# Expert outputs added to the residual rows in DRAM by the scatter, and a shorter last stage

## Chip, core and metric

One Trainium2 chip, one core. The metric is the device time of one execution in microseconds. The kernel before takes 815.87 us as the median of 3 runs (814.08 to 816.09).

## What is computed

One layer of a hybrid encoder for 512 prompt tokens and 32 sample tokens (544 rows of 1024 f32): a modulated RMS norm, a projection into two groups of heads (a gated linear recurrence and a forgetting attention), an output projection with a gated residual, then a grouped mixture of experts with a gated residual and a last RMS norm. The change touches what comes after the output projection:

```
def moe(h, w_router, b_router, w_gate, w_up, w_down):
    ...
    y = jnp.zeros((B * L, D), jnp.float32)
    for e in range(N_EXPERTS):
        he = jax.nn.silu(t @ w_gate[e]) * (t @ w_up[e])
        y = y + gates[:, e:e + 1] * (he @ w_down[e]).astype(jnp.float32)
    return y.reshape(B, L, D).astype(h.dtype)

    # in trunk_layer: x is the residual after the output projection ("x2"), h its modulated norm ("h2")
    x = x + gate_f * moe(h, p['w_router'], p['b_router'], p['w_exp_gate'][l], p['w_exp_up'][l], p['w_exp_down'][l])
    # at the end: rms_norm(x, final_norm_gain)
```

There are 16 experts of width 512; each token goes to exactly 2 of them. An expert's three weight matrices are 6.3 MB in f32, so all experts are 100 MB.

## The kernel before, in words

**Routing.** `route` (line 1098, on DVE) ranks the experts of each token, counts the tokens of each expert (a PE step, "pos"), and gives each of the 1088 token-expert pairs a place in a list of tiles of 32 rows, at least 2 tiles an expert. One-hot matrices (`row_hot`, `tile_hot`, `tile_entry`, lines 1163 to 1168) and 20 matmuls ("tab", line 2019) turn that into `tseq`, a table that holds for each tile two indices: the row of `h2_d` to gather from and the row of `y_d` to write to. `h2_d` holds the 544 rows of h2 in DRAM; `y_d` has 1088 rows, the first expert's output of a token in its first half, the second's in its second. A further 20 matmuls ("gates", line 2028) make the router's weight of each place.

**The tile loop.** This input has 44 tiles. A tile's 32 tokens stand on 128 partitions, four quarters of 256 elements a token. For tile t:

- POOL issues the gather, an indirect DMA of 128 rows of 1 KB (line 838), two tiles ahead of its use, into one of two buffers.
- DVE rearranges them (`reorder_rows`, line 1561), and transposes them (`turn_rows`, line 1565) when PE is done with the tile before.
- PE multiplies with the gate and up weights (line 2042, 128 matmuls recorded as 64), ACT applies silu (line 1084), DVE multiplies (line 1580) and transposes the product (line 1588).
- PE multiplies with the down weights (line 2053), behind the next tile's gate and up matmuls.
- DVE multiplies the result with the router's weight and the modulation gate (lines 1593 to 1597, then the eviction in `y_out`, line 1602) into one of two `ysb` buffers.
- POOL issues the scatter (line 844) of 128 rows of 1 KB to `y_d`.

The order on each engine is written out by hand. DVE, in pass t: turn rows t+1, hidden product t, **reorder rows t+2**, factors, transpose hidden t, evict y t-1. POOL, in turn: gather n+4 (after DVE has reordered n+2), scatter n (after its eviction, and after the scatter from the same buffer, n-2, has landed). PE: gate and up of t, then down of t-1.

**Weights.** SP loads experts in 6 pieces of 1 MB, each issued when the piece four before it has landed, into 4 expert buffers. The loads of expert e wait for the last tile of expert e-4.

**The last stage.** SP loads x2 rows of row tiles 0 and 4 while the last tiles run. When all scatters have landed it loads 10 pieces of `y_d` (lines 651 and 652), two for each of the 5 row tiles. For row tiles 0 and 4 DVE adds them to x2; for 1, 3 and 2 PE adds them with an identity matrix (line 2085) onto x2, which 12 matmuls at line 2001 put in PSUM just after routing began. ACT squares and sums, DVE takes the root (`rstd`, three Newton steps) in three groups, and scales; SP stores.

Of the kernel before, what the change touches and what calls it, by code (L numbers as in the profile page):

```python
# [18 lines left out]
I32 = mybir.dt.int32  # L19
# [19 lines left out]
MAXT = 2 * NE + 2 * TOK // ET  # L39
# [22 lines left out]
def build(nc, a, out):  # L62
    ctx = ExitStack()
    with ctx:  # L64
# [109 lines left out]
        y_d = dram("y_d", (2 * TOK, D))  # L174
# [105 lines left out]
        grp("tab", 6, "dve")  # L280
        grp("gates", 6, "dve")
# [76 lines left out]
        s_xsum = sem("x2_in_psum")  # L358
        s_xr = sem("x2_reloaded")
# [116 lines left out]
        gA, gB = view(R, T0 + 912, NTILE), view(R, T0 + 920, NTILE)  # L476
# [8 lines left out]
        quarter_i = view(R, T0 + 1050, 1).bitcast(I32)  # L485
        quarter = view(R, T0 + 1443, 1)
        quarter_out = view(R, T0 + 1051, 1)
# [6 lines left out]
        entry = view(R, T0 + 1464, 2 * NTILE, 2)  # L494
        iota_r = view(R, T0 + 1484, P)
        iota_t = view(R, T0 + 1484 + P, MAXT + 2)

        tseq = view(XH, 8960, MAXT + 2, 2).bitcast(I32)
        row_hot = view(R, 1920, 2 * NTILE, P)
        tile_hot = view(R, 3200, 2 * NTILE, MAXT + 2)  # L500
        tile_entry = view(R, 0, 2 * NTILE, MAXT + 2, 2)

        ya = [view(W, 6 * SLOT + n * D, D) for n in range(NTILE)]
        yb = [view(W, 6 * SLOT + (NTILE + n) * D, D) for n in range(NTILE)]
        gateF = view(XH, 8192, 2, QD)
# [52 lines left out]
        def _(sp):  # L558
# [39 lines left out]
            first_pieces(0, (2, 3))  # L598
            first_pieces(1, (0, 1))
# [41 lines left out]
            for i in (0, 4):  # L641
                sp.dma_start(xr[i][0:ROWS[i], :], x2_d[i * P:i * P + ROWS[i], :]).then_inc(s_xr, 16)
# [5 lines left out]

            def load_y(i):
                n = ROWS[i]  # L650
                sp.dma_start(ya[i][0:n, :], y_d[i * P:i * P + n, :]).then_inc(s_ya[i], 16)  # L651
                sp.dma_start(yb[i][0:n, :], y_d[TOK + i * P:TOK + i * P + n, :]).then_inc(s_ya[i], 16)  # L652

            for i in FIN:
                load_y(i)
            for m, i in enumerate(FIN):
                n = ROWS[i]
                sp.wait_ge(s_fin, m + 1)
                sp.dma_start(out["y_prompt"][0, i * P:i * P + n, :] if i < 4 else out["y_sample"][0],
                             ya[i][0:n, :]).then_inc(s_out[m % 2], 16)  # L660
# [8 lines left out]
        def _(pool):  # L669
# [140 lines left out]
            g.iota(iota_r, [[0, P // ET], [1, ET]], base=0, channel_multiplier=0, allow_small_or_imprecise_dtypes=True)  # L810
            g.iota(quarter_i, [[0, 1]], base=0, channel_multiplier=1)
            g.iota(iota_t, [[1, MAXT + 2]], base=0, channel_multiplier=0, allow_small_or_imprecise_dtypes=True)
            for c in range(2):
                g.iota(entry[:, c * NTILE:(c + 1) * NTILE, 0], [[P, NTILE]], base=-8 * TOK, channel_multiplier=1,
# [1303 lines left out]
```

## Time and profile before

| what | value |
|---|---|
| median of 3 runs | 815.87 us |
| the profiled execution, its own time | 812.85 us |
| its span | 811.1 us |
| PE busy | 688.7 us (85%) |
| DVE / ACT / POOL busy | 382.1 / 207.5 / 203.9 us |
| routing, first one-hot matrix to the first gate matmul | 485.1 to 504.4 us |
| tile loop, first gate matmul to the last eviction | 504.4 to 776.2 us |
| last stage, last scatter landed to the end | 779.4 to 811.1 us |

Times inside the profile count from the start of the span. 1.8 us of the execution lie outside the span. PE, DVE, ACT, POOL and SP run on their own and wait for each other through semaphores; a wait shows as idle time of an engine before an instruction, with the instruction or DMA that ended it.

### The profile page before, as it was taken

How to read it: one execution, taken by the hardware profiler on the slowest of the kernel's cores; microseconds unless marked ns; L12 is line 12 of the kernel's file. 1: busy time of each engine (PE TensorE's matmuls, PEld its weight loads, DVE VectorE, ACT ScalarE, POOL GpSimd, SP SyncE). 2: the span in 40 equal slices, each digit the busy share in tenths (PEclk: the TensorE clock that was granted, in tenths of full speed). 3: DMA queues.
4: the chain of work that ended last, by engine and by line, in shares of the span. 5: the costliest groups of instructions: out<-in, count | busy, mean ns of one | idle time of the engine just before them, and what ended most of it. 6: DMA issues, size and time to landing. Idle time of an engine off the chain costs nothing. (4 is left out here: it accounts for less than half of the span.)

```text
span 811.1 us, 18872 instructions
## 1 busy us (share of the span) xinstructions
PE 688.7 (85%) x7369; PEld 434.6 (54%) x7370; DVE 382.1 (47%) x1063; ACT 207.5 (26%) x429; POOL 203.9 (25%) x338
## 2 busy tenths in 40 slices
PE   3699999999787789998899955998889988979925
PEld 1385485444244678666645534665556655656712
DVE  4200025011497898666635483344445444455546
ACT  5300145001422142566111100222222232223202
POOL 1212200001842610311000001343334344434410
PEclk9799999999989999998799975999999999999978
DMA  8953074364104100950770187899995999972053
GB/s 330 390 236 104 26 286 183 130 227 176 68 17 144 45 2 6 330 187 5 306 304 27 49 321 304 323 416 416 417 418 204 415 421 413 415 321 97 30 194 155
DMA packets 37540, 179.59 MB, mean 221 GB/s; under 512 B 5816, under 2 KB 6216, under 8 KB 21808
## 3 DMA queue, kind: packets, MB, share of 16 engines
q1 hardware_dynamic: 29536, 157.31, 49.0%
q0 software_dynamic: 7952, 21.55, 7.6%
q8 instruction: 38, 0.62, 0.3%
q14 instruction: 14, 0.11, 0.0%
HBM read 168.00 MB, written 13.71 MB: 224 GB/s over the span
## 5 line engine op out<-in xcount | busy, mean ns | idle before, releaser
L1754 PE MATMUL bank<-weights,x_hT 128*128 128x512 f32 x256 | 113.3, 601 | 0.0
L1738 PE MATMUL bank<-x_hT,weights 128*128 128x272 f32 x384 | 91.7, 400 | 2.0 <-DMA weights<-in_w_in 2.0
L2042 PE MATMUL bank<-weights,R 128*32 128x256 f32 x1408 | 83.1, 388 | 11.9 <-DVE R L1565 5.7
L1738 PEld LDWEIGHTS bank<-x_hT,weights 128*128 128x128 f32 x384 | 73.9, 194 | 18.5 <-DMA weights<-in_w_in 2.4
L1754 PEld LDWEIGHTS bank<-weights,x_hT 128*128 128x128 f32 x256 | 48.7, 193 | 60.3 <-issue 60.1
L844 POOL DMA_INDIRECT y_d<-R,x_hT x44 | 45.1, 1024 | 123.6 <-DVE R L1602 110.1
L2042 PEld LDWEIGHTS bank<-weights,R 128*32 128x32 f32 x1408 | 54.7, 112 | 37.3 <-issue 10.8
L1084 ACT ACTIVATE R<-bank 128x128 f32<-128x128 f32 x44 | 12.2, 277 | 205.7 <-PE bank L2042 205.7
L1084 ACT ACT_TABLE_LOAD x44 | 56.5, 1283 | 22.6 <-DVEq L1191 21.8
L838 POOL DMA_INDIRECT R<-h_d,x_hT x46 | 49.2, 1070 | 37.6 <-POOL x_hT L856 32.1
L1964 PE MATMUL bank<-weights,x_hT 128*128 128x512 f32 x128 | 56.9, 596 | 0.0
L1561 DVE COPY R<-R 128x256 f32 (+1 forms) x46 | 18.6, 404 | 75.0 <-DMA R<-h_d,x_hT 72.8
L2053 PE MATMUL bank<-R 128*32 128x256 f32 x704 | 44.2, 391 | 9.4 <-DVE R L1602 9.2
L2053 PE MATMUL bank<-weights,R 128*32 128x256 f32 x704 | 42.6, 380 | 9.3 <-DVE R L1602 9.2
L2042 PE MATMUL bank<-R 128*32 128x256 f32 x704 | 40.3, 379 | 3.1 <-issue 3.1
L2042 PE MATMUL bank<-x_hT,R 128*32 128x256 f32 x704 | 40.3, 379 | 2.5 <-issue 2.5
L2053 PEld LDWEIGHTS bank<-R 128*32 128x32 f32 x704 | 26.8, 112 | 24.3 <-issue 15.6
L2053 PEld LDWEIGHTS bank<-weights,R 128*32 128x32 f32 x704 | 25.8, 109 | 24.2 <-issue 15.5
L1565 DVE STREAM_TRANSPOSE R<-R 128x256 f32<-128x256 f32 x45 | 20.1, 446 | 38.5 <-PE bank L2042 36.5
L1964 PEld LDWEIGHTS bank<-weights,x_hT 128*128 128x128 f32 x128 | 23.6, 190 | 26.4 <-issue 26.3
L1718 PE MATMUL bank<-weights,cpad 128*32 128x512 f32 x192 | 25.0, 648 | 14.7 <-DMA weights<-in_w_ada 14.7
L1266 DVE COPY weights<-bank 128x272 f32<-128x272 f32 x8 | 3.2, 437 | 70.4 <-PE bank L1738 70.2
(353 smaller groups left out, 997.2 us busy)
## 6 DMA issues: line engine op xcount, KB each, us to landing
weights<-in_w_ada SPq DMA_DIRECT2D x24, 1024.0 KB, 11.8
weights<-in_w_exp_gate SPq DMA_DIRECT2D x16, 1024.0 KB, 10.2
weights<-in_w_exp_down SPq DMA_DIRECT2D x16, 1024.0 KB, 10.4
weights<-in_w_exp_up SPq DMA_DIRECT2D x16, 1024.0 KB, 10.9
R<-in_w_exp_down SPq DMA_DIRECT2D x16, 1024.0 KB, 10.5
weights<-in_w_in SPq DMA_DIRECT2D x7, 2048.0 KB, 8.8
R<-in_w_exp_up SPq DMA_DIRECT2D x8, 1024.0 KB, 10.7
R<-in_w_exp_gate SPq DMA_DIRECT2D x8, 1024.0 KB, 10.4
```

The source lines that it names most:

```text
L838: pool.indirect_dma_start(xg[:, par * QD:(par + 1) * QD], None, h2_quarters, bass.IndirectOffsetOnAxis(ap=gather_rows[par], axis=0), bound ...
L844: pool.indirect_dma_start(y_quarters, bass.IndirectOffsetOnAxis(ap=scatter_rows[par], axis=0), ysb[:, par * QD:(par + 1) * QD], None, boun ...
L1084: A.activation(hs, bank[2][:, 0:P], ACT.Silu).then_inc(s_sil, 1)
L1266: read("dve", f"hf{h}{c}", V.tensor_copy(fr[:, c * HALF:(c + 1) * HALF], bank[4 + 2 * (h % 2) + c][:, 0:HALF]))
L1561: V.tensor_copy(xsort, xg[:, bass.ds(place * QD, QD)].rearrange("p (r b) -> p b r", b=KT)).then_inc(s_xs, 1)
L1565: V.transpose(XT.rearrange("p b r -> p (b r)"), xsort.rearrange("p b r -> p (b r)")).then_inc(s_xt, 1)
L1718: ins = T.matmul(bank[b][32 * j:32 * j + 32, :], cpad[:, k, :], w[:, j * 512:(j + 1) * 512], start=(k == 0), stop=(k == KT - 1))
L1738: ins = T.matmul(bank[b][:, 0:HALF], w[:, k, h * P:(h + 1) * P], hT[:, k, c * HALF:(c + 1) * HALF], start=(n == 0), stop=(n == KT - 1))
L1754: ins = T.matmul(bank[b][:, :], hT[:, k, i * P:(i + 1) * P], w[:, k, :], start=(k == 0), stop=(k == KT - 1))
L1964: ins = T.matmul(b[:, :], hT[:, k, i * P:(i + 1) * P], wslot(f"wo{k // 2}", D)[:, k % 2, c * 512:(c + 1) * 512], start=(k == 0), stop=(k = ...
L2042: ins = T.matmul(bank[2][32 * j:32 * j + 32, 0:2 * P].rearrange("p (w f) -> p w f", w=2), XT[:, k, :], W2[:, :, k, j * P:(j + 1) * P], sta ...
L2053: ins = T.matmul(bank[6][32 * j:32 * j + 32, 0:QD], heT[:, f, :], Wd[:, f, j * QD:(j + 1) * QD], start=(f == 0), stop=(f == FT - 1))
```

## The change

- `y_d` is gone. All five x2 row tiles are stored to `x2_d` (before, two). The scatter goes to `x2_d` with `compute_op=ALU.add`, so that the DMA adds the 128 rows to what is there.
- Since both experts of a token now add to the same row, each scatter waits for the scatter before it to have landed, not for the one before that.
- Gather and scatter use one index, so `tseq` and the one-hot matrices are smaller: 32 columns in place of 128. The table comes out on 32 partitions and DVE writes it in four pieces. The first two gathers take their index from `tseq` itself and start when it has been written.
- In the DVE loop `reorder_rows(t + 2)` stands behind `y_out(t - 1)`.
- SP issues the 8 gate broadcasts earlier, and the first piece of expert 2's gate weights only when the first two gathers have landed.
- The last stage loads 5 pieces of `x2_d`. DVE multiplies them with the gain while ACT squares, one root for all five, then DVE scales three row tiles and ACT two. PE has no part; the 12 matmuls at line 2001 and the 12 adds at line 2085 (24 rows in the profile) are gone.

```
-MAXT = 2 * NE + 2 * TOK // ET
+MAXT = 2 * NE + 2 * TOK // ET - 2
...
+            for gi in range(2):
+                for j in range(4):
+                    sp.dma_start(gateF[32 * j:32 * j + 32, gi, :], bcast(mod_d[gi, 5 * D + j * QD:5 * D + (j + 1) * QD], 32)).then_inc(s_ph3, 16)
             first_pieces(1, (0, 1))
...
-            sp.wait_ge(s_x2w, 32)
-            sp.wait_ge(s_xsum, 1)
+            sp.wait_ge(s_x2w, 16 * NTILE)
             first_pieces(3, (2, 0, 1))
             both(sp, s_h2w)
+            for n in range(2):
+                sp.wait_ge(s_gath[n], 16)
             first_pieces(2, (0,))
...
-            def load_y(i):
...
             for i in FIN:
-                load_y(i)
+                sp.dma_start(xr[i][0:ROWS[i], :], x2_d[i * P:i * P + ROWS[i], :]).then_inc(s_xr[i], 16)
...
             def scatter(par):
                 pool.sem_inc(s_begun, 1)
-                pool.indirect_dma_start(y_quarters, bass.IndirectOffsetOnAxis(ap=scatter_rows[par], axis=0),
+                pool.indirect_dma_start(x2_quarters, bass.IndirectOffsetOnAxis(ap=scatter_rows[par], axis=0),
                                         ysb[:, par * QD:(par + 1) * QD], None,
-                                        bounds_check=last_y, oob_is_err=False).then_inc(s_yst[par], 16)
+                                        bounds_check=last_quarter, oob_is_err=False, compute_op=ALU.add).then_inc(s_yst[par], 16)
...
             def next_scatter(u, par):
-                if not isinstance(u, int):
-                    pool.wait_ge(s_yst[par], u * 16)
-                g.tensor_copy(scatter_rows[par], tseq[:, bass.ds(u * 2 + par, 1), 1]).then_inc(s_idx, 1)
+                g.tensor_copy(scatter_rows[par], tseq[:, bass.ds(u * 2 + par, 1)]).then_inc(s_idx, 1)
                 pool.wait_ge(s_ye, u * 2 + (par + 2))
+                if par:
+                    pool.wait_ge(s_yst[0], u * 16 + 16)
+                elif not isinstance(u, int):
+                    pool.wait_ge(s_yst[1], u * 16)
...
-            V.tensor_tensor(row_hot, iota_r.unsqueeze(1).broadcast_to([P, 2 * NTILE, P]),
-                            dst_r.unsqueeze(2).broadcast_to([P, 2 * NTILE, P]), ALU.is_equal)
...
+            vlink(dve, V.tensor_tensor(row_hot, iota_r.unsqueeze(1).broadcast_to([P, 2 * NTILE, ET]),
+                                       dst_r.unsqueeze(2).broadcast_to([P, 2 * NTILE, ET]), ALU.is_equal))
+            V.tensor_tensor(row_entry, row_hot, entry.unsqueeze(2).broadcast_to([P, 2 * NTILE, ET]), ALU.mult)
+            V.tensor_tensor(tile_hot, iota_t.unsqueeze(1).broadcast_to([P, 2 * NTILE, MAXT + 2]),
+                            dst_t.unsqueeze(2).broadcast_to([P, 2 * NTILE, MAXT + 2]), ALU.is_equal).then_inc(s_oh, 1)
...
@@ hidden(t)
-                reorder_rows(t + 2, t % 2)
@@ block.vector
             with dve.Fori(5, total) as t:
                 hidden(t)
                 gate_factors(t)
...
                 y_out(t - 1, (t - 1) % 2)
+                reorder_rows(t + 2, t % 2)
...
+            for m, i in enumerate(FIN):
+                n = ROWS[i]
+                dve.wait_ge(s_xr[i], 16)
+                V.tensor_tensor(yr[i][0:n, :], xr[i][0:n, :], fing[0:n, :], ALU.mult).then_inc(s_gain, 1)
+            dve.wait_ge(s_fsq, NTILE)
+            rstd(st[:, 105:110], st[:, 100:105], D)
+            dve.wait_ge(s_gain, NTILE)
+            dve.sem_inc(s_root, 1)
+            for m in (0, 2, 4):
+                n = ROWS[FIN[m]]
+                y = yr[FIN[m]][0:n, :]
+                V.tensor_scalar(y, y, st[0:n, 105 + m:106 + m], None, ALU.mult).then_inc(s_fin["dve"], 1)
```

On POOL, the second half of the loop's body, before. `rows_reordered` is DVE's step at line 1561, `y_evicted` the one at line 1602, `y_stored0` and `y_stored1` tell of landed scatters from the two buffers:

```order
L856 ISA [waits rows_reordered]
L856 COPY x_hT<-x_hT 128x1
L879 REGISTER_ALU
L838 DMA R<-h_d,x_hT 128x256 [waits index_copied]
L862 ISA [waits y_stored1]
L862 COPY x_hT<-x_hT 128x1
L863 REGISTER_ALU
L882 REGISTER_ALU [waits y_evicted]
L844 DMA y_d<-R,x_hT 4352x256 [waits index_copied]
```

The same place in the changed kernel:

```order
L835 ISA [waits rows_reordered]
L835 COPY x_hT<-x_hT 128x1
L860 REGISTER_ALU
L816 DMA R<-h_d,x_hT 128x256 [waits index_copied]
L839 ISA
L839 COPY x_hT<-x_hT 128x1
L840 REGISTER_ALU
L842 REGISTER_ALU [waits y_evicted]
L863 REGISTER_ALU [waits y_stored0]
L822 DMA x_d<-R,x_hT 2176x256 [waits index_copied]
```

The wait for a landed scatter has moved from ahead of the index copy to just ahead of the scatter, and from the same buffer's last scatter (two tiles back) to the other buffer's (one tile back).

On DVE, the loop's body before, from the hidden product on:

```order
L1580 TENSOR_TENSOR R<-R,bank 128x32x4 [waits silu_done,xT_ready]
L1558 ISA
L1560 ISA [waits rows_gathered0]
L1561 ISA [waits rows_gathered1]
L1561 COPY R<-R 128x256
L1593 ISA [waits rows_reordered]
L1593 COPY stats<-R 128x2
...
L1588 STREAM_TRANSPOSE R<-R 128x128 [waits down_done,hidden_ready,gate_factor_step]
L1621 ISA [waits hiddenT_ready]
L1622 ISA [waits y_stored0]
L1602 ISA [waits y_stored1]
L1602 TENSOR_TENSOR R<-bank,x_hT 128x256
```

And in the changed kernel:

```order
L1555 TENSOR_TENSOR R<-R,bank 128x32x4 [waits silu_done,xT_ready]
L1567 ISA
L1567 COPY stats<-R 128x2
...
L1562 STREAM_TRANSPOSE R<-R 128x128 [waits down_done,hidden_ready,gate_factor_step]
L1599 ISA [waits hiddenT_ready]
L1600 ISA [waits y_stored0]
L1576 ISA [waits y_stored1]
L1576 TENSOR_TENSOR R<-bank,x_hT 128x256
L1533 ISA
L1535 ISA [waits rows_gathered0]
L1536 ISA [waits rows_gathered1]
L1536 COPY R<-R 128x256
```

The wait for the gathered rows of tile t+2 stood ahead of the factors, the hidden transpose and the eviction; it now stands behind all three.

## Rows read from the trace of the kernel before

**Rows 1.** The page: span, busy time of each engine.
```profile
span 811.1 us, 18872 instructions
PE 688.7 (85%) x7369; PEld 434.6 (54%) x7370; DVE 382.1 (47%) x1063; ACT 207.5 (26%) x429; POOL 203.9 (25%) x338
```
**Rows 2.** Scatters (line 844) in stretches of the loop: us, POOL busy (x count), PEclk, DMA share, GB/s.
```profile
515.50:616.50 101.00, 16.42 (x16) 0.98 1.00 406
...
625.70:726.60 100.90, 16.68 (x17) 1.00 0.99 403
726.60:769.00 42.40, 7.18 (x7) 1.00 0.21 67
```
**Rows 3.** POOL in time order, 651 to 663 us: start, us, instruction, idle before.
```profile
651.96 1.06 POOL L838 DMA_INDIRECT R<-h_d,x_hT  x1 [0.79 <-POOL x_hT L856]
656.15 1.02 POOL L844 DMA_INDIRECT y_d<-R,x_hT  x1 [2.94 <-DVE R L1602]
658.17 1.06 POOL L838 DMA_INDIRECT R<-h_d,x_hT  x1 [0.79 <-POOL x_hT L856]
662.46 1.02 POOL L844 DMA_INDIRECT y_d<-R,x_hT  x1 [3.03 <-DVE R L1602]
```
**Rows 4.** DVE in time order, the same stretch.
```profile
658.64 0.40 DVE L1561 COPY R<-R 128x256 f32 x1 [2.42 <-DMA R<-h_d,x_hT]
661.14 0.42 DVE L1602 TENSOR_TENSOR R<-bank,x_hT 128x256 f32 x1 [0.53 <-DVE R L1588]
664.58 0.40 DVE L1561 COPY R<-R 128x256 f32 x1 [1.94 <-DMA R<-h_d,x_hT]
```
**Rows 5.** Waits of DVE, 515 to 727 us: total, times, longest.
```profile
DVE R L1561 <- DMA R<-h_d,x_hT: 63.2, 31, 3.5
```
**Rows 6.** PE in time order after the weights have landed, 727 to 766 us.
```profile
727.23 3.66 PE L2042 MATMUL bank<-weights,R 128*32 128x256 f32 x64 [0.71 <-issue]
...
760.55 3.66 PE L2042 MATMUL bank<-x_hT,R 128*32 128x256 f32 x64
765.73 3.66 PE L2042 MATMUL bank<-x_hT,R 128*32 128x256 f32 x64
```
**Rows 7.** The chain that ended last: the last scatter.
```profile
777.07 2.36 DMA y_d<-R,x_hT
```
**Rows 8.** Routing, 474 to 504 us, in time order.
```profile
473.86 0.49 DVE L1114 TENSOR_TENSOR R<-R 128x320 f32<-128x320 f32 x1
485.11 1.48 DVE L1163 TENSOR_TENSOR R<-R 128x1280 f32<-128x1280 f32 x1
486.51 0.86 DVE L1165 TENSOR_TENSOR R<-R 128x680 f32<-128x680 f32 x1
487.40 1.57 DVE L1167 TENSOR_TENSOR R<-R 128x1360 f32<-128x1360 f32 x1
489.12 4.00 PE L2019 MATMUL bank<-R 128*128 128x136 f32 x20 [8.43 <-DVE R L1167]
493.24 0.36 DVE L1189 TENSOR_SCALAR x_hT<-bank,R 128x136 int32<-128x136 f32 x1 [1.07 <-PE bank L2019]
495.85 1.13 POOL L838 DMA_INDIRECT R<-h_d,x_hT  x1 [0.90 <-POOL x_hT L849]
503.44 0.39 DVE L1561 COPY R<-R 128x256 f32<-128x256 f32 x1 [8.77 <-DMA R<-h_d,x_hT]
```
**Rows 9.** The last stage, 779 to 808 us, in time order.
```profile
779.51 0.32 SPq L651 DMA_DIRECT2D weights<-y_d  x1
785.39 1.22 DVE L1635 TENSOR_TENSOR weights<-weights 128x1024 f32<-128x1024 f32 x1 [9.19 <-DMA weights<-y_d]
787.90 1.06 ACT L1096 ACTIVATE weights<-weights 128x1024 f32<-128x1024 f32 x1 [18.17 <-DVE weights L1636]
808.08 0.33 SPq L659 DMA_DIRECT2D out_y_prompt<-weights  x1
```
**Rows 10.** A group by line: a scaling of row tiles, x5, one of them 32 rows.
```profile
L1236 DVE TENSOR_SCALAR weights<-x_hT,stats 128x1024 f32<-128x1024 f32 (+1 forms) x5 | 3.7, 749 | 2.3 <-PE bank L1727 2.2
```

More of the change, by code:

```diff
@@ L279, in build @@
         grp("pos", 6, "dve")
[L280 to L281 removed]
+        grp("tab", 5, "dve")
+        grp("gates", 4, "dve")
         pe_done = sem("pe_done")
@@ L1087, in _ @@
                 n = ROWS[i]
+                act.wait_ge(s_xr[i], 16)
                 if m:
                     act.wait_ge(s_fsq, m)
-                if i in psums:
-                    act.wait_ge(s_part, m - 1)
-                    alink(act, A.activation(jk[0:n, 0:512], bank[psums[i][0]][0:n, :], ACT.Square, accum_out=st[0:n, 100 + m:101 + m]))
-                    A.activation(jk[0:n, 512:D], bank[psums[i][1]][0:n, :], ACT.Square, accum_out=st[0:n, 130 + m:131 + m]).then_inc(s_fsq, 1)
-                else:
-                    act.wait_ge(s_comb, m + 1)
-                    A.activation(jk[0:n, :], xr[i][0:n, :], ACT.Square, accum_out=st[0:n, 100 + m:101 + m]).then_inc(s_fsq, 1)
+                A.activation(jk[0:n, :], xr[i][0:n, :], ACT.Square, accum_out=st[0:n, 100 + m:101 + m]).then_inc(s_fsq, 1)
+            act.wait_ge(s_root, 1)
+            for m in (1, 3):
+                n = ROWS[FIN[m]]
+                y = yr[FIN[m]][0:n, :]
+                A.activation(y, y, ACT.Identity, scale=st[0:n, 105 + m:106 + m]).then_inc(s_fin["act"], 1)
         def route(dve, V, last_h2):
@@ L1183, in route @@
             vlink(dve, V.tensor_tensor(t80[3], t80[3], gts, ALU.mult))
-            V.tensor_reduce(gA, t80[3], AX.X, ALU.add)
+            V.tensor_reduce(weights2[:, 0:NTILE], t80[3], AX.X, ALU.add)
             vlink(dve, V.tensor_tensor(t80[4], gts, t80[3], ALU.subtract))
-            vlink(dve, V.tensor_reduce(gB, t80[4], AX.X, ALU.add))
+            vlink(dve, V.tensor_reduce(weights2[:, NTILE:], t80[4], AX.X, ALU.add))
             filled(dve, "tab")
-            tb = bank[6][:, 0:2 * (MAXT + 2)].rearrange("p (t c) -> p t c", c=2)
-            read("dve", "tab", V.tensor_scalar(tseq, tb, 4.0, quarter_out, ALU.mult, ALU.add))
+            for j in range(P // ET):
+                ins = V.tensor_scalar(tseq[j * ET:(j + 1) * ET, :], bank[5][0:ET, 0:MAXT + 2], 4.0, float(32 * TOK + j), ALU.mult, ALU.add)
+            read("dve", "tab", ins)
             taken(dve, "tab")
             dve.sem_inc(s_rd, 1)
-            for c, weight in ((0, gA), (1, gB)):
-                ins = V.tensor_tensor(tile_hot[:, c * NTILE:(c + 1) * NTILE, :], tile_hot[:, c * NTILE:(c + 1) * NTILE, :],
-                                      weight.unsqueeze(2).broadcast_to([P, NTILE, MAXT + 2]), ALU.mult)
-            ins.then_inc(s_tg, 1)
+            V.tensor_tensor(row_weight, row_hot, weights2.unsqueeze(2).broadcast_to([P, 2 * NTILE, ET]), ALU.mult).then_inc(s_tg, 1)
         @block.vector
@@ L1604, in _ @@
             filled(dve, "gates")
-            read("dve", "gates", V.tensor_copy(row_gate[:, :, 1:], bank[6][:, 0:2 * (MAXT + 2)].rearrange("p (g t) -> p g t", g=2)))
+            for j in range(P // ET):
+                ins = V.tensor_copy(row_gate[j * ET:(j + 1) * ET, :, 1:], bank[4][0:ET, 0:2 * (MAXT + 2)].rearrange("p (g t) -> p g t", g=2))
+            read("dve", "gates", ins)
             taken(dve, "gates")
@@ L1995, in _ @@
             router(4, 1)
-            pe.wait_ge(s_x2, 2 * NTILE)
-            for i, places in psums.items():
-                for c, b in enumerate(places):
-                    taken(pe, last[b])
-                    ins = T.matmul(bank[b][:, :], ident[:, :], x[:, i, c * 512:(c + 1) * 512], start=True, stop=False)
-            ins.then_inc(s_xsum, 1)
             begin("pos")
@@ L2079, in _ @@
             down(3, total)
-            for i in FIN[2:]:
-                places = psums[i]
-                pe.wait_ge(s_ya[i], 32)
-                for c, b in enumerate(places):
-                    for src in (ya, yb):
-                        ins = T.matmul(bank[b][:, :], ident[:, :], src[i][:, c * 512:(c + 1) * 512], start=False, stop=(src is yb))
-                ins.then_inc(s_part, 1)
 _INS = ['x_prompt', 'x_sample', 'cache_fox_k', 'cache_fox_v', 'cache_fox_logf', 'state_hgrn', 'c_prompt', 'c_sample',
```

155 lines of the change are left out of this document (50 added, 105 removed).

## The prediction

> **What bounds the kernel now.** I start from the page: PE is busy 85% of the span [rows 1]. That is a mean over stages with different limits, so I read the three stages that the change touches one by one: routing, the tile loop, the last stage.
>
> For the tile loop I cut the time where the weight stream starts and stops [rows 2]. In two stretches, 201.9 us together, the DMA engines are busy all the time (share 1.00 and 0.99, above 400 GB/s), and 33 scatters begin: 6.12 us a tile. Where the weights are done, one gate-and-up group follows the other every 5.18 us [rows 6]; that is PE's own pace, 5.5 us with the changes of expert (7 intervals from 727.2 to 765.7 us [rows 6]). So in four fifths of the loop PE is not the bound.
>
> What is? The waits say it: in that time DVE waits 31 times, 63.2 us in all, for gathered rows [rows 5]. One gather starts at 651.96 [rows 3], and DVE, which waits for it, starts its reorder at 658.64 [rows 4]: 6.7 us, some 6.2 of it the transfer and the rest DVE's waking and the second wait (the other pairs in this stretch give 6.3 to 6.7). The reader is to see a ring: rows landed, reorder at 658.64, eviction at 661.14 to 661.56, which stands behind the reorder on DVE, scatter 0.90 later at 662.46, then the next gather 2.0 to 2.3 later, then 6.2 again. That is about 12.3 us, and since gathers alternate between two buffers it is 6.15 us a tile. The row count gave 6.12.
>
> **The tile loop after the change.** Two edits work against each other here.
>
> The reorder goes behind the eviction. That cuts the ring: the eviction no longer waits for the gather. A gather would then start some 3 us after the eviction (0.90 + 1.02 + 1.0 [rows 3, 4]) and land 6.2 later, 9.2 us in all, against the two tiles (10.4 us at PE's pace) that it has. The 6.15 us bound is gone, and alone this edit would let the loop run near 5.5 us a tile.
>
> The scatter now waits for the one before it to have landed. It is issued by POOL, so everything behind it on POOL waits too: the next index copy and the next gather. The ring is: scatter starts, lands after L, POOL issues the next one 0.90 after what releases it (661.56 to 662.46 [rows 3, 4]). So the pace is L + 0.9. With nothing else on the DMA engines L is 2.36 us [rows 7], which makes 3.3 us, hidden behind 5.18. But beside the weights no row shows L of a scatter. The nearest row is the gather of the same 128 rows of 1 KB: 6.2 us. The plain write can hardly be much faster than this, since its packets queue behind the same weight packets; I take 5.9 as the lower end. The add must also read the target rows. At the measured 406 GB/s those 128 KB are 0.3 us, and if every row is handled as a transfer of its own the queueing behind weights repeats, which could double the 3.8 us that the load adds (6.2 - 2.4): L up to 10. No row has an add, so this is the term most likely off. I take L = 6.5, near the row: 6.2 + 0.3. The pace is 7.4 us a tile beside the weights.
>
> The weights need the same 201.9 us. In that time there are now 201.9 / 7.4 = 27.3 tiles in place of 33; the other 5.7 follow at 5.5 us: +31 us. Two `ysb` buffers let PE run on for a tile at the start of each stretch and POOL catch up at 3.3 us after it; I estimate 3 us back for each of the two: **+25 us**.
>
> **Routing.** Three one-hot steps of 1.48, 0.86 and 1.57 us become two of 320 elements, 0.49 each, and one of 0.86 [rows 8]: 2.0 us less. The 20 matmuls (4.0 us) get a 32-column stationary operand; I take 2.5, between 2.0 and 4.0, but DVE's other steps behind the one-hots (3.3 us, 488.9 to 492.2) then end last, and four small reads of about 0.25 replace the 0.36 one. So the table is done 2.4 us earlier than 493.60. The gather needs no copy of its index: it starts 0.9 after the table in place of 2.25 (493.60 to 495.85). Together 3.75 us. It took 7.6 us to the reorder at 503.44, with a weight piece and 8 broadcasts just ahead of it on the queues; those are moved, and I take 6.4 as elsewhere: 1.2 more. **-4.9 us**, between -3.7 and -6.5. The 8 broadcasts now take SP 3.7 us near 468 us, where pieces wait for earlier ones anyway. The three more x2 stores are POOL and DMA work before routing, while POOL waits for DVE; the 12 identity matmuls ended at 478.3, before the mask that "pos" waits for at 479.1. I cost all three at nothing. If the DMA engines had no room there, the weight pieces would shift by the 1.5 MB, 3.7 us, ahead of tiles that need them only 20 us later.
>
> **The last stage.** Before: last scatter landed at 779.43, end at 811.1, 31.7 us. After, from the last landing: five issues of 0.45 us on SP, 2.2 MB in place of 4.5. Last piece landed at about +7.8 (2.2 MB at 406 GB/s, and 2.4). ACT squares of 1.06 + 0.2 [rows 9] keep pace, last at +9.1; DVE's gains, 5 of 1.22 [rows 9], end at +9.5. The root is 12 steps of 0.2: +11.9. DVE scales three (0.75 each [rows 10]), ACT two: +14.2. Five stores, 2.2 MB, begin at +12.8, and the DMA needs 5.4 us and a start of 1.7: +19.9. **-11.8 us**, between -9 and -14. The last two scatters began 2.7 us apart (774.37 and 777.07); now the ring of 2.36 + 0.3 + 0.9 = 3.6 spaces them, and the last one itself takes 0.3 more: **+1**.
>
> **Sum**, against the profiled execution's 812.85: -4.9 - 11.8 + 1 + 25 = +9, so 822 us. The runs' median (815.87) lies 3.0 above that execution; on their scale **825 us**. What a measurement can tell from no change is about 0.3%, 2.5 us.
>
> **The rule that speaks the other way.** The trace shows L = 2.36 us without load and 6.2 with it [rows 3, 4, 7]. The Trainium skill ("DMA: Bandwidth & Descriptors", Anatomy of one DMA, SWDGE path) gives one formula for a transfer issued by GpSimd, 2.0 us and the bytes at 436 GB/s, which is 2.3 us here whatever else runs. The row without load agrees, the rows beside the weights do not. By that formula the sum would be the first rival's.
>
> **Rivals.**
>
> *The serial scatter stays hidden, faster.* If a scatter lands within 4.3 us even beside the weights, L + 0.9 is below 5.18 and only the good edit is left. The loop gains perhaps 10 us, not the full 33 x 0.6, since the weight stream (201.9 us) then holds it up. 812.85 - 15.7 - 10 = 787, 790 on the runs' scale. Against it: every gather took 6.2. For it: a write need not wait for a read from DRAM. Chance 0.09.
>
> *The add is free, L = 5.9 to 6.2.* Pace 6.9: 29.3 tiles, 3.7 displaced at 5.5 is 20, less 6, +14. With the other terms 811, and 814 on the runs' scale; with L a little smaller, or more given back by the buffers, 805. This is the point that decides the sign: above L of 6.1 it is slower, below it faster. Chance 0.27, two thirds of it faster.
>
> *The add is dear.* Row by row, L = 8.5: pace 9.4, 21.5 tiles, 11.5 displaced, +63 less 6: 854, 857 on the runs' scale. Then POOL's gathers, queued behind the waiting scatter, come late too. Chance 0.20, from L = 7.5 (843) on.
>
> *My forecast*, L 6.3 to 7.3: 821 to 840. Chance 0.44.
>
> **Numbers.** Faster is the first rival (0.09) and most of the second (0.19): 0.28. Within 0.3%: 0.07, from the second. Slower: 0.65. The range leaves out the first rival and about half of the dear case, 0.19 together: 800 to 852.
>
> **What would show it.** Scatter starts 7 to 8 us apart beside the weights and about 5.2 behind them; POOL's idle time before the scatter ended by the DMA to x2, not by DVE's eviction; DVE's waits for gathers well below 63 us, and its waits before the eviction for a landed scatter instead. First gate matmul near 499.5; from the last landing to the end about 20 us. I am wrong if scatters stay 6.1 apart or closer in the two stretches (then L is smaller than a gather's), or if POOL's scatter instruction itself grows far beyond 1.02 us, which would put the price on POOL and not on the DMA.

## The result, and where the time went

The changed kernel takes **850.1 us** (median of 4 runs, 848.25 to 852.26), the kernel before in the same session 816.0; the ratio is 1.041, 95% interval [1.037, 1.046]. The profiled execution took 851.36 us, span 849.6.

The page and the waits of the changed kernel:

```profile
span 849.6 us, 18805 instructions
PE 684.7 (81%) x7333; PEld 429.8 (51%) x7334; DVE 367.8 (43%) x1037; ACT 209.0 (25%) x425; POOL 229.4 (27%) x336
...
q0 software_dynamic: 12608, 23.13, 10.5%
...
PE 47%; DMA 28%; DVE 11%; issue 7%; ACT 3%; POOL 2%; POOLq 1%; SPq 1%; ACTq 0%; DVEq 0%
```

PE works as long as before (684.7 us against 688.7 [rows 1]), in a longer span. In the chain that ended last, DMA has 28%, and 23% is one kind of transfer, the scatter into x2.

The trace is cut at three instants that every kernel here has: the start of the two "pos" matmuls in routing, the first gate matmul, the landing of the last scatter.

| stage, us | before | after | difference | forecast |
|---|---|---|---|---|
| "pos" to first gate matmul | 25.2 | 21.0 | -4.1 | -4.9 |
| loop, to the last scatter landed | 275.1 | 324.4 | **+49.4** | +26 |
| last stage, to the end | 31.7 | 20.5 | -11.1 | -11.8 |
| sum | | | +34.1 | +9 |

The sum is the difference of the medians (850.1 - 816.0). The two profiles differ by 4.4 us more, because "pos" began at 483.62 in place of 479.21. That is no part of the change: in seven executions of kernels whose code up to there is that of the changed kernel but for a few stores (experiments 1, 2, 5, 6, 7, 9, 10 below), it began between 477.5 and 487.7. Each stage time here and below is that of one profiled execution; the medians are over 4 executions or more.

**The loop.** Scatters (line 822) of the changed kernel in stretches: us, POOL busy (count), PEclk, DMA share, GB/s.

```profile
515.00:605.00 90.00, 16.03 (x10) 0.96 0.97 372
605.00:617.00 12.00, 3.30 (x2) 1.00 0.31 71
617.00:635.00 18.00, 3.19 (x2) 0.81 0.95 365
635.00:650.00 15.00, 4.93 (x3) 1.00 0.34 58
650.00:765.00 115.00, 24.38 (x15) 0.91 0.91 349
765.00:828.00 63.00, 19.11 (x12) 0.98 0.28 45
```

Where before there were 33 scatters in 201.9 us of steady stream [rows 2], there are now 10 in 90 us, and the stream itself has holes: in two of them (605 to 617, 635 to 650) SP waits for a buffer that PE has not released, and between them the granted clock is 0.81. The scatter's own row is in the chain of waits (start, us):

```profile
518.70 9.13 DMA x_d<-R,x_hT
...
528.65 8.88 DMA x_d<-R,x_hT
...
548.88 8.22 DMA x_d<-R,x_hT
...
558.00 8.47 DMA x_d<-R,x_hT
...
820.90 3.63 DMA x_d<-R,x_hT
...
825.38 3.69 DMA x_d<-R,x_hT
```

Beside the weights 16 of them take 8.2 to 9.6 us, mean 8.83; behind the weights 3.4 to 3.9. And POOL, in time order, shows the ring:

```profile
528.65 1.60 POOL L822 DMA_INDIRECT x_d<-R,x_hT  x1 [5.99 <-DVE R L1576]
...
531.25 1.07 POOL L816 DMA_INDIRECT R<-h_d,x_hT  x1 [0.80 <-POOL x_hT L835]
...
538.41 1.60 POOL L822 DMA_INDIRECT x_d<-R,x_hT  x1 [5.89 <-DMA x_d<-R,x_hT]
```

From scatter to scatter 9.8 us: 8.88 until it has landed, then 0.9 until POOL issues the next. The gather goes out 2.6 us behind the scatter. The waits from 515 to 765 us (total, times, longest):

```profile
POOL x_d L822 <- DMA x_d<-R,x_hT: 89.4, 19, 6.6
DVE R L1576 <- DMA x_d<-R,x_hT: 76.6, 24, 6.3
DVE R L1536 <- DMA R<-h_d,x_hT: 38.2, 25, 5.2
PE bank L2000 <- DVE R L1576: 29.8, 14, 4.4
```

DVE waits less for gathered rows, 38.2 us in this stretch of 250 us against 63.2 in one of 212 [rows 5], and twice as long before the eviction (L1576) for a scatter. PE's down matmul waits for that eviction.

**Routing**, in time order:

```profile
483.62 0.71 PE L1957 MATMUL bank<-R 128*128 128x96 f32 x2 [7.88 <-issue]
484.13 2.21 PE L1959 MATMUL bank<-R 128*128 128x80 f32 x10
...
489.85 0.49 DVE L1141 TENSOR_TENSOR R<-R 128x320 f32<-128x320 f32 x1
...
494.84 0.91 DVE L1166 TENSOR_SCALAR x_hT<-bank 32x66 int32<-32x66 f32 x4
...
496.76 1.13 POOL L816 DMA_INDIRECT R<-h_d,x_hT  x1 [9.84 <-issue]
...
503.72 0.39 DVE L1536 COPY R<-R 128x256 f32<-128x256 f32 x1 [7.34 <-DMA R<-h_d,x_hT]
...
504.65 1.94 PE L1989 MATMUL bank<-weights,R 128*32 128x256 f32 x16 [5.74 <-DVE R L1540]
```

One-hots to table: 489.85 to 495.75, 5.9 us, against 8.5 [rows 8]. The gather starts 1.0 us behind the table, against 2.25, and 6.96 us later the reorder begins, against 7.6.

**The last stage**, in time order:

```profile
829.15 2.23 SPq L639 DMA_DIRECT2D weights<-x_d  x5
...
833.30 5.01 DVE L1615 TENSOR_TENSOR weights<-weights 128x1024 f32<-128x1024 f32 x4 [0.59 <-DMA weights<-x_d]
...
837.09 1.06 ACT L1072 ACTIVATE weights<-weights 128x1024 f32<-128x1024 f32 x1
...
840.82 2.07 DVE L1623 TENSOR_SCALAR weights<-weights,stats 32x1024 f32<-32x1024 f32 x3 [0.19 <-DVE stats L1192]
...
841.98 2.99 SPq L643 DMA_DIRECT2D out_y_prompt<-weights  x4
```

The landing is at 829.07; squares end at +9.2, the root at +11.6, scaling at +13.8, the span at +20.5. That is the forecast's schedule, within 0.6 us at every step.

### The profile page after: what moved, and what is told of

Read it like the earlier page. It is cut to its first block, busy times and chain, and to the rows that moved or that the text cites. A ratio compares the mean times of both kernels' runs of the same rounds, so it can differ in the third digit from the quotient of the medians.

```text
span 849.6 us, 18805 instructions
## 1 busy us (share of the span) xinstructions
PE 684.7 (81%) x7333; PEld 429.8 (51%) x7334; DVE 367.8 (43%) x1037; ACT 209.0 (25%) x425; POOL 229.4 (27%) x336
## 3 DMA queue, kind: packets, MB, share of 16 engines
q0 software_dynamic: 12608, 23.13, 10.5%
## 4 chain that ended last, share of the span: by engine, by line
PE 47%; DMA 28%; DVE 11%; issue 7%; ACT 3%; POOL 2%; POOLq 1%; SPq 1%; ACTq 0%; DVEq 0%
DMA x_d<-R,x_hT 23%; PE bank L1693 10%; PE bank L1709 10%; PE bank L1919 6%; PE bank L1989 5%; DMA weights<-in_w_in 2%; PE bank L1673 2%; PE bank L2000 2%; DMA R<-h_d,x_hT 2%; DMA weights<-in_w_ada 1%; PE bank L1638 1%; PE bank L1682 1%; PE bank L1866 1%; PE bank L1712 1%; DVE weights L1342 1%
## 5 line engine op out<-in xcount | busy, mean ns | idle before, releaser
L1709 PE MATMUL bank<-weights,x_hT 128*128 128x512 f32 x256 | 113.0, 600 | 0.0
L822 POOL DMA_INDIRECT x_d<-R,x_hT x44 | 70.9, 1612 | 147.5 <-DMA x_d<-R,x_hT 92.1
L1989 PE MATMUL bank<-weights,R 128*32 128x256 f32 x1408 | 86.1, 399 | 21.7 <-DVE R L1555 12.6
L1989 PEld LDWEIGHTS bank<-weights,R 128*32 128x32 f32 x1408 | 55.2, 115 | 51.0 <-DVE R L1540 21.3
L2000 PE MATMUL bank<-R 128*32 128x256 f32 x704 | 45.5, 400 | 21.0 <-DVE R L1576 21.0
L1919 PE MATMUL bank<-weights,x_hT 128*128 128x512 f32 x128 | 59.5, 618 | 0.0
L1576 DVE TENSOR_TENSOR R<-bank,x_hT 128x256 f32 (+1 forms) x44 | 18.7, 424 | 85.8 <-DMA x_d<-R,x_hT 78.2
L2000 PE MATMUL bank<-weights,R 128*32 128x256 f32 x704 | 45.0, 396 | 10.9 <-DVE R L1576 10.9
L1989 PE MATMUL bank<-R 128*32 128x256 f32 x704 | 44.5, 409 | 7.9 <-DVE R L1555 6.6
L2000 PEld LDWEIGHTS bank<-R 128*32 128x32 f32 x704 | 26.7, 115 | 37.1 <-issue 28.2
L2000 PEld LDWEIGHTS bank<-weights,R 128*32 128x32 f32 x704 | 27.4, 114 | 24.6 <-issue 14.8
L1989 PEld LDWEIGHTS bank<-R 128*32 128x32 f32 x704 | 27.0, 118 | 24.4 <-issue 8.3
## 6 DMA issues: line engine op xcount, KB each, us to landing
weights<-in_w_exp_down SPq DMA_DIRECT2D x16, 1024.0 KB, 11.1
```

The source lines that it names most:

```text
L822: pool.indirect_dma_start(x2_quarters, bass.IndirectOffsetOnAxis(ap=scatter_rows[par], axis=0), ysb[:, par * QD:(par + 1) * QD], None, bou ...
L1576: V.tensor_tensor(ysb[:, bass.ds(place * QD, QD)], bank[6][:, 0:QD], factor, ALU.mult).then_inc(s_ye, 1)
L1709: ins = T.matmul(bank[b][:, :], hT[:, k, i * P:(i + 1) * P], w[:, k, :], start=(k == 0), stop=(k == KT - 1))
L1919: ins = T.matmul(b[:, :], hT[:, k, i * P:(i + 1) * P], wslot(f"wo{k // 2}", D)[:, k % 2, c * 512:(c + 1) * 512], start=(k == 0), stop=(k = ...
L1989: ins = T.matmul(bank[2][32 * j:32 * j + 32, 0:2 * P].rearrange("p (w f) -> p w f", w=2), XT[:, k, :], W2[:, :, k, j * P:(j + 1) * P], sta ...
L2000: ins = T.matmul(bank[6][32 * j:32 * j + 32, 0:QD], heT[:, f, :], Wd[:, f, j * QD:(j + 1) * QD], start=(f == 0), stop=(f == FT - 1))
```

## The experiments

The theory: the loop's pace beside the weights is L + 0.9, and L of an add is 8.8, not 6.5. Rivals: the chain of waits costs by itself, whatever L; the add loads POOL or the DMA engines; the reorder's place matters more or less than thought. All results at once; "loop" and the rest are cut as above, L is the mean over the scatters beside the weights, ratios with 95% intervals.

| kernel | scatter | L | loop | "pos" to gate | last stage | median | ratio to before |
|---|---|---|---|---|---|---|---|
| before | plain, two in flight, reorder ahead | 6.14 | 275.1 | 25.2 | 31.7 | 816.0 | 1 |
| after | add, serial, reorder behind | 8.83 | 324.4 | 21.0 | 20.5 | 850.1 | 1.041 [1.037, 1.046] |
| 1 | plain, serial, behind | 6.27 | 289.0 | 21.1 | 20.5 | 817.1 | 0.999 [0.995, 1.003] |
| 2 | add, two in flight, behind | 8.47 | 257.6 | 20.9 | 20.5 | 779.9 | 0.956 [0.951, 0.961] |
| 3 | before, reorder behind | 6.03 | 253.4 | 24.7 | 31.3 | 794.7 | 0.975 [0.970, 0.980] |
| 4 | before, serial | 6.27 | 293.5 | 25.1 | 33.7 | 843.1 | 1.033 [1.025, 1.041] |
| 5 | add, serial, reorder ahead | 8.89 | 332.4 | 20.9 | 20.6 | 862.1 | 1.057 [1.052, 1.061] |
| 6 | as 1, quarters apart | 6.29 | 290.3 | 21.3 | 21.6 | 818.8 | 1.000 [0.997, 1.004] |
| 7 | as 2, summed, 10 loads | 8.54 | 257.7 | 21.2 | 28.6 | 790.0 | 0.968 [0.964, 0.972] |
| 8 | as 3, with the change's routing | 6.29 | 253.5 | 20.1 | 32.4 | 789.0 | 0.965 [0.962, 0.969] |
| 9 | after, 64 of 128 rows | 7.21 | 301.9 | 20.9 | 20.8 | 827.0 | 1.015 [1.007, 1.022] |
| 10 | 1, 64 of 128 rows | 5.85 | 275.4 | 21.5 | 21.1 | 803.6 | 0.988 [0.981, 0.995] |

L runs from the start of POOL's instruction to the last landing of that scatter, and its mean is over the scatters that take more than three quarters of the longest. The kernel before was run again in every session; its own median was 816.0 beside the changed kernel, 816.3 beside 1 to 4, 818.5 beside 5 to 8 and 812.7 beside 9 and 10, so the ratios compare better than the medians. "pos" to gate repeats within 0.6 us among the kernels with the same code there; the last stage within 1.1 us where it has five loads and within 2.4 us where it is that of before. So these two terms stand on several executions each.

### 1. The add taken away, the serial wait kept

```diff
-  bounds_check=last_quarter, oob_is_err=False, compute_op=ALU.add).then_inc(s_yst[par], 16)
+  bounds_check=last_quarter, oob_is_err=False).then_inc(s_yst[par], 16)
```

> The changed kernel with the scatter writing its rows in place of adding them (it leaves out the sum of the two expert outputs and x2: the last writer of a row stays); the wait for the scatter before and everything else are kept. Theory A (the price is the add itself, which handles the rows one by one, 128 packets of 1 KB in place of 32 of 4 KB): the scatter beside the weights lands after 5.9 to 6.2 us in place of 8.2 to 9.6, POOL's instruction falls from 1.61 to 1.02 us, the pace beside the weights is about 6.9 us a tile in place of 9 to 10, and the time is 812 to 820. Theory B (the price is the chain of waits on POOL, which makes gathers and weight pieces late whatever the scatter does): the scatters stay 8 us apart or more and the time stays above 838.

Theory A holds: 817.1 us, though L (6.27) and the pace (7.21) are a little above what it gave. Chain and page of this kernel:

```profile
558.75 5.99 DMA x_d<-R,x_hT
...
565.62 6.27 DMA x_d<-R,x_hT
```
```profile
q0 software_dynamic: 8384, 23.12, 8.2%
```

The software queue carries 8384 packets against 12608 with the add, 4224 fewer for 44 scatters: 96 each, which is 128 packets against 32; the sizes in the packets' records, 1024 and 4096 bytes, say the same. The add on top of a serial wait costs 35.4 us of loop.

### 2. The add kept, the serial wait taken away

```diff
-  if par:
-      pool.wait_ge(s_yst[0], u * 16 + 16)
-  elif not isinstance(u, int):
-      pool.wait_ge(s_yst[1], u * 16)
...
-  pool.indirect_dma_start(x2_quarters,
+  pool.indirect_dma_start(x2_quarters[par],
```

The scatter two before has to have landed, as in the kernel before, and the second target is a second array, z2_d, a copy of x2.

> The changed kernel with its adds sent alternately to x2 and to a second copy of x2 in DRAM, each scatter waiting only for the one two before it (it leaves out the sum of the two copies, and pays five more stores of x2). Theory A (what costs is that one add stands behind the other, L + 0.9 a tile, while an add in the background is affordable): pace beside the weights 6.1 or below, time 788 to 806. Theory C (the add's single-row packets themselves fill the DMA engines or POOL, however they are ordered): the scatters land later still, 10 us or more, the weight stream falls below 380 GB/s, pace 7 us or more, time above 815.

779.9 us, below theory A's range. Theory C falls. Scatters in the steady stream of this kernel:

```profile
520.00:600.00 80.00, 23.42 (x15) 1.00 1.04 397
660.00:720.00 60.00, 17.56 (x11) 1.00 1.04 396
```

Its adds land as late as those of the changed kernel (8.47), POOL's instruction is 1.6 us as there, and yet a tile takes 5.6 us (35 intervals from 513.2 to 710.9). What is late harms nobody when nobody waits for it. The bill of packets shows only in the stream, 396 to 397 GB/s against 410 to 416 in experiment 3, and in 4.2 us of loop.

### 3. The reorder alone

```diff
 def hidden(t):
...
-    reorder_rows(t + 2, t % 2)
...
     y_out(t - 1, (t - 1) % 2)
+    reorder_rows(t + 2, t % 2)
```

> The kernel before with one edit, the rows' reorder put behind the eviction; scatter plain, two in flight. Theory A (the gather ring of 12.3 us for two tiles was the bound beside the weights, so this edit is worth what the prediction gave it): 33 tiles in 201.9 us become about 36 at 5.5 to 5.6 us, 3 to 4 tiles fewer behind the weights at 5.2, time 796 to 804. Theory D (the weight stream itself was the bound, the gather ring only filled its gaps): the stream ends at the same time, tiles that are done early wait for the next expert's weights, time 811 to 816.

794.7 us: theory A, 1.3 us below its range. The same windows for this kernel:

```profile
520.00:600.00 80.00, 15.39 (x15) 1.00 1.01 416
660.00:720.00 60.00, 11.29 (x11) 1.00 1.01 410
```

Experiments 1, 2, 3 and the changed kernel are the four corners of one table (loop, reorder behind in all):

| | two in flight | serial |
|---|---|---|
| plain | 253.4 | 289.0 |
| add | 257.6 | 324.4 |

An add costs 4 us, a serial wait 36, the two together 71. The change bought 21.7 us with the reorder (275.1 to 253.4) and lost 71. Each of these loops is one execution. The medians, less the kernel's own "pos" to gate and last stage, say nearly the same of the add alone, the wait alone and both: 0, 37 and 70 us; for the reorder they say 20.

### 4. The serial wait alone

```diff
   pool.wait_ge(s_ye, u * 2 + (par + 2))
+  if par:
+      pool.wait_ge(s_yst[0], u * 16 + 16)
+  elif not isinstance(u, int):
+      pool.wait_ge(s_yst[1], u * 16)
```

> The kernel before with one edit, each plain scatter waits until the one before it has landed; reorder still ahead of the eviction. Theory A (serial scatters cost L + 0.9 = 6.9 us a tile beside the weights and hold back the gather queued behind them, so the gather ring grows too): pace 7 to 8, time 832 to 850. Theory E (a serial wait on a 6 us write hides in the 6.12 us pace apart from the 0.9): pace 6.9, time 822 to 830. If it costs less than 5 us, the wait alone is no part of the loss.

843.1 us, as theory A has it, pace 7.24. The waits of this kernel, 515 to 765 us:

```profile
POOL y_d L844 <- DMA y_d<-R,x_hT: 103.4, 27, 4.7
DVE R L1565 <- DMA R<-h_d,x_hT: 82.2, 30, 4.8
```

The loop of the profiled execution grows by 18.4 us, and its last stage by 2.0; the median grows by 26.8, so a single loop can be off by some us here. The gathers, queued behind the waiting scatter, come later too: 82.2 us of DVE's waits against 63.2 [rows 5].

### 5. The reorder put back ahead, in the changed kernel

```diff
 def hidden(t):
...
+    reorder_rows(t + 2, t % 2)
...
     y_out(t - 1, (t - 1) % 2)
-    reorder_rows(t + 2, t % 2)
```

> The changed kernel with the reorder put back ahead of the eviction. Theory A (in the changed kernel the ring of scatters binds beside the weights, L + 0.9 = 9.9 us a tile or 19.9 for two, and the gather ring of 12.3 us for two tiles has 7 us of room in it): the reorder's place is worth almost nothing, time 846 to 856. Theory F (the reorder's place is worth the 21.7 us that it was in the kernel before, whatever else binds): 866 to 874.

862.1 us lies between the two. The loop is 8.0 us longer, somewhat over a third of what the reorder was worth in experiment 3, so most of its worth is hidden by the scatter ring, but not all. DVE's waits for gathers (515 to 765 us) are 111.4 us against 38.2:

```profile
DVE R L1536 <- DMA R<-h_d,x_hT: 111.4, 28, 6.7
```

That the remaining 8 us arise where L is short and the gather ring binds again was not tried.

### 6. The quarters of a token apart

```diff
-  h2_d = dram("h2_d", (TOK, D))
-  x2_d = dram("x2_d", (TOK, D))
+  h2_d = dram("h2_d", (4 * TOK, QD))
+  x2_d = dram("x2_d", (4 * TOK, QD))
...
-  bank[5][0:ET, 0:MAXT + 2], 4.0, float(32 * TOK + j), ALU.mult, ALU.add)
+  bank[5][0:ET, 0:MAXT + 2], 1.0, float(8 * TOK + j * TOK), ALU.mult, ALU.add)
```

> The kernel of the plain serial write (it leaves out the sum, as there), with h2 and x2 laid out in DRAM so that the four quarters of a token lie in four places, 1 KB each, in place of one place of 4 KB. Theory P (what makes the add slow is only that its rows go as 128 packets of 1 KB): the plain scatter lands after 8 to 9 us beside the weights too, the gathers get slower likewise, and the time is 840 to 855. Theory A (the read and the sum make it slow; 1 KB packets of a plain write do not): L stays 5.9 to 6.5, time 814 to 824.

818.8 us and L 6.29, so theory A's numbers; but the run doesn't decide what it was made for. The software queue has 8384 packets here as in experiment 1:

```profile
q0 software_dynamic: 8384, 23.12, 8.3%
```

A plain scatter puts four rows into a packet wherever they go. The run shows that neighbouring addresses do not matter; it does not part the packets from the add. Experiments 9 and 10 do that, read together with the packets' records.

### 9 and 10. Half the rows, added and plain

```diff
-  bass.IndirectOffsetOnAxis(ap=scatter_rows[par], axis=0),
-  ysb[:, par * QD:(par + 1) * QD], None,
+  bass.IndirectOffsetOnAxis(ap=scatter_rows[par][0:P // 2], axis=0),
+  ysb[0:P // 2, par * QD:(par + 1) * QD], None,
```

This is the edit of 9; 10 leaves out `compute_op` too.

> The changed kernel with only the first 64 of the 128 rows of each tile added (it leaves out half of the columns of every expert output); all waits kept. Theory Q (an add's packets stand one behind the other in each DMA engine's queue among the weight packets, 8 to an engine; between the plain scatter's 6.27 us and the add's 8.83 the extra packets cost some 0.4 us each): with 4 to an engine the add lands after 7.0 to 7.6 us beside the weights, POOL's instruction falls below 1.61 us, and the time is 826 to 838. Theory X (an add has a fixed extra latency, whatever its size): it lands after 8.5 us or more and the time stays above 842.

> The same with 64 of 128 rows, written plainly in place of added (it leaves out half of the columns of every expert output and the sum). Theory Q (two data packets to an engine become one): 5.8 to 6.1 us beside the weights in place of 6.27, time 811 to 817. Theory Y (beside the weights a scatter's time goes with its bytes): about half of the 3.8 us that the load adds goes, 4.4 us, and the time falls below 808.

Chain rows, first of the kernel that adds, then of the plain one:

```profile
650.83 7.22 DMA x_d<-R,x_hT
...
658.93 7.03 DMA x_d<-R,x_hT
```
```profile
662.03 5.44 DMA x_d<-R,x_hT
...
668.35 5.48 DMA x_d<-R,x_hT
```

The means are 7.21 and 5.85, both inside what theory Q gives. The times say less: 827.0 is inside its range, 803.6 below it, where theory Y had put it. But the 4.4 us that theory Y asks of L did not come, and theory Q's range was badly worked: 0.42 us of L comes back at each of some 33 tiles, 13.9 us, and the loop fell by 13.6. The page counts 9792 and 7680 packets in the software queue, 2112 apart for 44 scatters, 48 each: 64 against 16. Four points, by data packets in each of the 16 engines:

| packets per engine | 1 (plain) | 2 (plain) | 4 (add) | 8 (add) |
|---|---|---|---|---|
| L beside the weights, us | 5.85 | 6.27 | 7.21 | 8.83 |
| 5.45 + 0.42 per packet | 5.87 | 6.29 | 7.13 | 8.81 |

One line holds plain and added ones. But half the packets are also half the bytes, so the line alone does not part a price by the packet from one by the added byte. The trace of the changed kernel does. Its 44 tiles have 1408 places for 1088 pairs; the row of an empty place is skipped, and by the packets' records it goes out as a packet all the same, of 8 bytes. Every scatter has 128 packets. The one at 548.88 adds 24 rows, the one at 558.00 all 128. The software queue while they were under way (548.9 to 557.1, 558.0 to 566.5 us; gathers included):

```profile
q0 software_dynamic: 187, 0.03, 3.1%
```
```profile
q0 software_dynamic: 187, 0.25, 13.4%
```

An eighth of the bytes in as many packets, and they land after 8.22 and 8.47 us. Of the 16 scatters beside the weights, the 7 with at most 60 rows to add (41 on the mean) take 8.63 us, the 9 with 120 or more 8.99; in experiment 5 it is 8.36 (6 scatters) and 9.18 (11). In experiment 9, with 64 packets, those with at least 60 of the 64 rows take 7.23 (13 scatters). So 41 rows in 128 packets take 1.4 us longer than some 64 rows in 64 packets: most of the price goes by the packets. The bytes have 0.4 to 0.8 us of it by these means.

The records also say when the packets go. The changed kernel's first one starts 4.8 us behind the start of POOL's instruction, the last at 8.1 (medians of the 16); without weights at 2.2 and 3.4. In experiment 1 it is 4.2 and 5.2, without weights 1.6 and 1.95 (its scatters and gathers have packets of the same sizes, so these are told apart by their order alone). The view from 558.2 to 562.5 us, with the scatter of 558.00 under way, has no packet of the software queue at all:

```profile
q1 hardware_dynamic: 246, 1.79, 100.4%
```

So 2.6 us of what the load costs stand ahead of the first packet, for either kind of scatter; what holds the first packet is not shown. The add's comes 0.6 us later than the plain one's, with and without weights, as much as POOL's instruction is longer (1.61 against 1.03). The 2.56 us between 6.27 and 8.83 are thus some 0.6 ahead of the first packet and 2 behind it, and the line is a fit to the totals. The add's price is for the most part that it goes out as one packet a row. What a packet waits for is seen in the DMA view of the changed kernel, 520 to 600 us (packets, MB, share of 16 engines):

```profile
q1 hardware_dynamic: 3905, 28.46, 87.1%
q0 software_dynamic: 1689, 1.64, 9.8%
```

A weight packet takes 0.871 x 16 x 80 / 3905 = 0.29 us, one of the software queue 0.07 us on the mean, together 0.36, near the slope of 0.42. That each packet waits for one of the other queue is worked out from this, not seen row by row. The Trainium skill ("DMA: Bandwidth & Descriptors", Queues, rings and completion order) says that an engine turns between its queues packet by packet; the line agrees.

### 7 and 8. Two versions that beat both kernels

7 is experiment 2 made whole: the second array is filled with zeros before the loop, and the last stage loads both and adds them.

```diff
+  sp.dma_start(z2_d[i * P:i * P + ROWS[i], :].rearrange("t (g d) -> t g d", g=8),
+               zeros[0:ROWS[i], :].unsqueeze(1).broadcast_to([ROWS[i], 8, D // 8])).then_inc(s_z, 16)
...
+  sp.dma_start(zr[i][0:ROWS[i], :], z2_d[i * P:i * P + ROWS[i], :]).then_inc(s_xr[i], 16)
...
+  V.tensor_tensor(xr[i][0:n, :], xr[i][0:n, :], zr[i][0:n, :], ALU.add).then_inc(s_sum, 1)
```

8 is experiment 3 with the change's routing and the order on SP, and a second small table for the scatter's index.

```diff
+  begin("tab2")
+  pe.wait_ge(s_oh, 2)
+  for j in range(2 * NTILE):
+      ins = T.matmul(bank[2][0:ET, 0:MAXT + 2], row_entry_y[:, j, :], tile_hot[:, j, :],
```

> Computes the reference: the changed kernel with adds that go alternately to x2 and to a second array in DRAM that is filled with zeros beforehand, each scatter waiting only for the one two before it; the end loads both and DVE adds them. Theory A: the 779.9 of the two unsummed targets, less two or three us of stores of x2, plus 2.2 MB of loads (5.5 us at 406 GB/s), and DVE keeps pace with 2.4 us a tile: 782 to 788. Theory G (DVE's five more adds and the doubled loads make the last stage as long as that of the kernel before, 31 us): 789 to 793, no better than the plain version with the reorder behind.

> Computes the reference: the kernel before (plain scatters to y, two in flight, its own last stage) with the reorder behind the eviction and with the change's routing: 32-column one-hots, first gathers straight from the table, the broadcasts early, and a second table for the scatter's index built behind the first. Theory A (the parts add up): 794.7 less the 4.1 us that routing gained in the changed kernel, 788 to 792. Theory H (routing's gain came from dropping the second index, so that with the second table it is lost): 793 to 796.

7 takes 790.0 us, two above theory A's range and within theory G's: the last stage is 28.6 us, 8.1 more than in experiment 2 and not 5.5, since SP now issues for 4.9 us and DVE's sum stands between each landing and ACT's square. 8 takes 789.0, as theory A has it, and theory H falls: the second table is built behind the first and costs nothing that the stages show. The two versions are not told apart (ratios 0.968 and 0.965, intervals overlap). Both beat the kernel before by 3.2 to 3.5% and the changed one by some 7%, and 8 needs no add.

## Why the prediction was right or wrong

- **The bound before, the gather ring: right.** Experiment 3 breaks it and gets 5.6 us a tile beside the weights (36 intervals from 520.3 to 721.7), the prediction's "near 5.5". The first rival priced the same edit at only 10 us, because the stream would hold the loop up; it was 21.7.
- **The new bound, L + 0.9: right.** 8.83 + 0.9 = 9.7 and 9.87 measured; 6.27 + 0.9 = 7.2 and 7.21 measured.
- **The step that failed: "I take L = 6.5, near the row: 6.2 + 0.3".** It was 8.83, so the pace was 9.9 us a tile and not 7.4. The 0.3 us for reading the target's bytes was the wrong thing to count: it is mostly the add's packets that cost, 8 to an engine in place of 2, some 2 us, and 0.6 comes ahead of the first of them. The prediction named that mechanism ("if every row is handled as a transfer of its own the queueing behind weights repeats"), bounded it at 10, and then chose the row of a transfer that goes four rows to a packet. The rows of before could have said this much: gathers and plain scatters were the only indirect transfers there, so no row could stand for an add. The dear rival, with L = 8.5 and a chance of 0.20, was the case that came.
- **The size: +9 us forecast, +34 measured.** That 850.1 lies inside the stated 800 to 852 is partly luck. The range took in about half of the dear case, and with L = 8.83 the prediction's own sum would have been some 861; the next error took 12 us off that.
- **From L to time: too dear.** By the formula L = 8.83 would be 201.9 / 9.73 = 20.7 tiles beside the weights, 12.3 displaced, +61 us; it was +49. For L = 6.27 it gives +21, and experiment 1 has +14. The 3 us given back per stretch were too little: with a slow loop the stream falls idle for a buffer, and in and next to those holes L is 3.4 to 5.5, and a tile takes about 5 us.
- **The last scatters, +1:** from 774.37 to the last landing at 779.43 it was 5.1 us, and from 820.90 to 829.07 it is 8.2: +3.1, inside the +49.
- **Routing, -4.9: -4.1.** One-hots and table -2.6 (forecast -2.4), no copy of the index -1.25 (-1.35), first gather -0.6 (-1.2), and 0.3 more ahead of the one-hots, on which see below.
- **Last stage, -11.8: -11.1**, with 20.5 to 20.6 us in the changed kernel and in experiments 1, 2 and 5.
- **What would show it:** POOL's idle time before the scatter is ended by the DMA, as said; DVE's waits moved from the gather to the scatter, as said. The first gate matmul was to come at 499.5 and came at 504.65, 4.4 of it the late "pos". Scatters were to start 7 to 8 us apart beside the weights and 5.2 behind them; it was 9.9 and 5.3. POOL's instruction did grow, from 1.02 to 1.61 us. Experiment 2 runs at 5.6 us a tile with it, so POOL's own time is not the bound; in a serial chain the 0.6 us is part of L.
- **The rule of the Trainium skill** ("DMA: Bandwidth & Descriptors", Anatomy of one DMA, SWDGE path) gives 2.0 us and the bytes at 436 GB/s, which is 2.3 for either scatter. Here it was 2.2 to 2.5 plain and 3.4 to 3.9 added without weights, 6.27 and 8.83 beside them. The trace agrees for the plain scatter without load alone.

## What to carry to other kernels

Price an indirect DMA beside a saturated stream by its packets per engine, not by its bytes, and an accumulating one as one packet a row; add what stands ahead of the first packet (4.2 to 4.8 us here, 1.6 to 2.2 without the stream). Before anything is made serial, ask what must really be ordered: a late transfer cost 4 us here when the next did not wait for it, 71 with the wait; where two writers may meet, a second target summed later is cheaper than a wait. And a change that bundles a good edit with a bad one should be taken apart: the reorder alone was worth 2.5%.

## What had not been expected

- **L is one line in the packets**, with the same slope for plain and added rows (0.42 us a packet and engine beside weights at about 400 GB/s), and an add of 24 rows, with 104 skipped, lands after 8.22 us, one of 128 rows after 8.47.
- **Four rows to a packet** in a plain scatter even when their targets are far apart (experiment 6).
- **The identity matmuls kept TensorE's clock up, in part.** The prediction costed the twelve (as the profile counts them) at nothing. In the profile of the kernel before they end at 478.3, 0.9 us ahead of "pos". Without them PE is idle for 7.88 us. The windows (PE busy, PEclk, DMA share, GB/s), first of after, then of before, then of experiment 3, whose code is that of before up to there, read:

```profile
483.00:487.00 4.00, 2.71 (x12) 0.50 1.00 422
```
```profile
479.00:483.00 4.00, 1.48 (x12) 0.86 0.66 246
```
```profile
481.90:485.00 3.10, 2.27 (x12) 0.60 0.70 296
```

In the changed kernel the granted clock is at the lower of its two levels, 1.2 GHz, and the twelve "pos" matmuls take 2.71 us against 1.48. But that profile of before is the exception: in experiments 3, 4 and 8, which keep the identity matmuls, PE was idle for 2.6 us ahead of "pos", and it took 2.27, 2.34 and 2.27 us. So what the twelve gave is 0.4 us in three executions and 1.2 in one. Experiment 8 comes from "pos" to the gate in 20.1 us against 20.9 to 21.5 of the others with this routing. It differs in more than that, so the 1 us is not shown to be the clock's alone.
